# Six places in place of eight for the gathered rows of the value stage

## The reference, cut to what matters

```
act = jax.nn.gelu(jnp.einsum('td,thkd->thk', hx, u[ex]))
out = jnp.einsum('thk,thkd->td', (gx.astype(act.dtype) * act), v[ex])
```

## Time and profile before

| | |
|---|---|
| median of 3 runs | 1711.44 us (1711.39, 1711.44, 1716.0) |
| the profiled execution, its own time | 1713.18 us |
| its span, first to last instruction | 1711.3 us |
| granted TensorE clock, mean | 0.978 |
| PE busy | 1621.1 us (95%) |
| DVE busy | 1064.0 us (62%) |
| POOL busy | 619.8 us (36%) |
| queue q0, the gathers | 268.47 MB |
| queue q1, SP's transfers | 208.06 MB |

### The profile page before, as it was taken

The page is one execution under the profiler, slowest core; times in us unless marked ns, Lnnn a source line. Parts: engine busy times, 40 slices in busy tenths (PEclk is TensorE's granted clock), DMA queues, the critical chain, the costliest instruction groups (busy, mean ns, idle before and its releaser), DMA issues.

```text
span 1711.3 us, 18283 instructions
## 1 busy us (share of the span) xinstructions
PE 1621.1 (95%) x6294; PEld 1052.1 (61%) x6294; DVE 1064.0 (62%) x2428; ACT 431.0 (25%) x1255; POOL 619.8 (36%) x650
## 2 busy tenths in 40 slices
PE   6988999998999799999989999999999999999957
PEld 3446454446588488888879999994444444444323
DVE  1010344442236999999968999997555556676772
ACT  3000444332011112111147777760000000000013
POOL 0000344460000144344445555555443344464620
PEclk9997999999999899999999999999999999999979
DMA  6231211004444699999989999999999999999940
GB/s 219 74 111 49 87 50 38 25 1 148 148 135 136 236 355 350 379 398 365 372 330 408 403 403 402 407 402 407 409 409 409 410 409 409 409 409 410 410 197 37
DMA packets 132552, 477.69 MB, mean 279 GB/s; under 512 B 14779, under 2 KB 15803, under 8 KB 132460
## 3 DMA queue, kind: packets, MB, share of 16 engines
q0 software_dynamic: 73728, 268.47, 40.0%
q1 hardware_dynamic: 58732, 208.06, 32.6%
HBM read 472.24 MB, written 4.24 MB: 278 GB/s over the span
## 4 chain that ended last, share of the span: by engine, by line
PE 65%; DMA 24%; DVE 4%; POOL 3%; issue 2%; ACT 1%; another core or an unknown queue 1%; SPq 0%; ACTq 0%; DVEq 0%
PE psum L1542 25%; DMA arena<-in_v,eidx 22%; PE psum L1453 6%; PE psum L1382 6%; PE psum L1272 5%; PE psum L1531 3%; PE psum L1415 3%; PE psum L1403 3%; PE psum L1489 2%; POOL arena L523 2%; PE psum L1340 2%; PE psum L1355 2%; PE psum L1295 1%; PE psum L1326 1%; PE psum L1285 1%
## 5 line engine op out<-in xcount | busy, mean ns | idle before, releaser
L1542 PE MATMUL psum<-arena 128*128 128x256 f32 x2048 | 455.2, 380 | 6.8 <-ACT arena L682 6.1
L1553 PE MATMUL psum<-arena 128*128 128x512 f32 x1024 | 440.8, 592 | 3.3 <-DMA arena<-in_vd 2.2
L523 POOL DMA_INDIRECT arena<-in_u,eidx x256 | 252.9, 988 | 474.7 <-DVE dots L1075 238.9
L1542 PEld LDWEIGHTS psum<-arena 128*128 128x128 f32 x2048 | 385.4, 191 | 57.4 <-issue 6.5
L523 POOL DMA_INDIRECT arena<-in_v,eidx x256 | 259.6, 1014 | 264.3 <-DVE arena L1110 147.8
L1553 PEld LDWEIGHTS psum<-arena 128*128 128x128 f32 x1024 | 194.2, 190 | 248.7 <-issue 242.5
L1110 DVE SCALAR_TENSOR_TENSOR arena<-arena,wts 128x1024 f32<-128x1024 f32 x182 | 233.2, 1285 | 118.9 <-DMA arena<-in_v,eidx 117.5
L1075 DVE CUSTOM_DVE_ANT_0 arena<-psum,arena 128x1024 f32<-128x1024 f32 x256 | 299.5, 1220 | 1.3 <-DVE arena L946 0.3
L501 POOL TENSOR_SCALAR arena<-arena 128x256 f32<-128x256 f32 (+4 forms) x128 | 105.9, 847 | 282.2 <-DVE arena L842 224.6
L1382 PE MATMUL psum<-arena 128*128 128x512 f32 x256 | 118.4, 605 | 0.0
L1453 PE MATMUL psum<-arena 128*128 128x256 f32 x512 | 113.0, 379 | 1.5 <-ACT arena L612 1.5
(11 more groups left out here) (175 smaller groups left out, 1400.6 us busy)
## 6 DMA issues: line engine op xcount, KB each, us to landing
arena<-in_ut SPq DMA_DIRECT2D x128, 512.0 KB
arena<-in_vd SPq DMA_DIRECT2D x128, 512.0 KB
arena<-in_wpack SPq DMA_DIRECT2D x105, 512.0 KB
arena<-in_u,eidx POOLq DMA_INDIRECT x256
arena<-in_v,eidx POOLq DMA_INDIRECT x256
arena<-in_w_pg SPq DMA_DIRECT2D x8, 512.0 KB
arena<-in_x SPq DMA_DIRECT2D x4, 512.0 KB, 4.9
arena<-bias_rows SPq DMA_DIRECT2D x8, 256.0 KB, 5.6
```

The source lines that it names most:

```text
L523: G.indirect_dma_start(out=row_slot(n), out_offset=None, in_=a["v"] if values else a["u"], in_offset=bass.IndirectOffsetOnAxis(ap=eidx[:, ...
L1542: last = T.matmul(chunk_scores(c), u[:, k * P:(k + 1) * P], h2T1[:, k, :], start=(k == 0), stop=(k == KC - 1))
L1553: last = T.matmul(ps[VALUE_BANK[t] + h], mixed[:, c, t * P:(t + 1) * P], stream[:, c % SRING, h * HALF:(h + 1) * HALF], start=(c == 0), st ...
```

## The change

From row 272 on, the gathered rows use only the six places at `SL`. Gather n then takes place (n - 272) mod 6. Gathers from n = 278 on wait until row n - 6 was used, those before (from n = 8) until row n - 8 was used. The two waits for `dense_scores` fall away, since nothing is gathered to `H2` any more. The functions `slot_of` and `slot_uses` give the place and how often its semaphore has been raised.

```diff
         low_slots = NG * COLS + -(-early_sums // SLOTS) * SLOTS
-        vslots = slots[:SLOTS - 2] + [place(H2 + i * D, [D])[0] for i in range(2)]
+        LATE_SLOTS = SLOTS - 2
+
+        def slot_of(n):
+            return n % SLOTS if n < low_slots else (n - low_slots) % LATE_SLOTS
+
+        def slot_uses(n):
+            return n // SLOTS + 1 if n < low_slots else low_slots // SLOTS + (n - low_slots) // LATE_SLOTS + 1
 
         def row_slot(n):
-            return (slots if n < low_slots else vslots)[n % SLOTS]
+            return slots[slot_of(n)]
...
-                if n >= SLOTS:
+                if n >= low_slots + LATE_SLOTS:
+                    pool.wait_ge(row_used, n - LATE_SLOTS + 1)
+                elif n >= SLOTS:
                     pool.wait_ge(row_used, n - SLOTS + 1)
-                if low_slots <= n < low_slots + SLOTS and n % SLOTS >= SLOTS - 2:
-                    pool.wait_ge(dense_scores, CHUNKS)
                 G.indirect_dma_start(out=row_slot(n), out_offset=None, in_=a["v"] if values else a["u"],
                                      in_offset=bass.IndirectOffsetOnAxis(ap=eidx[:, col:col + 1], axis=0)
-                                     ).then_inc(row_gathered[n % SLOTS], 16)
+                                     ).then_inc(row_gathered[slot_of(n)], 16)
...
-                dve.wait_ge(row_gathered[n % SLOTS], 16 * (n // SLOTS + 1))
+                dve.wait_ge(row_gathered[slot_of(n)], 16 * slot_uses(n))
```

## The result

The changed kernel is slower: 1718.26 us (median of 20 runs, 1714.82 to 1723.03) against 1712.56 us for the kernel before (20 runs, 1710.30 to 1717.36), ratio 1.0030, 95% interval 1.0021 to 1.0038. The medians differ by 5.7 us; the ratio makes it 5.1 us in 1712. The forecast was 1712.2 with a range to 1717.1. The profiled execution of the changed kernel took 1719.07 us, its span is 1717.3 (before: 1713.18 and 1711.3).

The account below looks back on a forecast made before the run. The prediction took the full DMA engines, up to the sum of row k = 120, as the bound. Transition 0.8 us plus three terms of 0 on the 1711.44 us median gave 1712.2 us, range 1708.3 to 1717.1.

Parts of the forecast that it names:

- What bounds the kernel: Value stage: DMA engines full until row k = 120 of the last tile is summed; the kernel's end follows that row.
- The transition: Start of six places: gather 278 waits for row 272, starting about 2.2 us later; cost 0 to 1.6, taken as 0.8 us.
- Rival C: At gather 278: the removed wait for dense scores pays, up to 3.1 us come back, 1708.3 us; chance 0.07.
- The mixed stretch: 1165 to 1620 us, dense stream beside gathered rows: six places give 12.3 us per round at 2.05 us a row; cost 0.
- The rows-only stretch: 1620 to 1641 us, after the dense stream: six places give a 7.68 us round at 1.28 us a row; cost 0.
- the 4.5 us above: A row's round without queueing: sum 1.28, GpSimd's reaction 0.27, issue until first bytes 1.67, own transfer 1.28 us.
- the upper bound of 4.1 us: After the stream: the whole 7.79 us trip taken as fixed, 1.51 us per row, 4.1 us lost over 18 rows.
- A: After the stream: the gather's trip is latency, not queueing; 4.1 us lost there, 1716.3 us in all; chance 0.08.
- B: Value stage: with fewer rows on order, fast DMA engines run dry before slow ones free a place; 1720.9 us, chance 0.09.

Follow-up runs that it names:

- early_tail: Kernel before, eight places, with the dense tiles' adds moved ahead in VectorE's order (tile 2's after k = 106, tile 3's after k = 109): 1694.80 us against 1712.96, ratio 0.9894.

## Why the prediction was wrong

- *What bounds the kernel.* Right: the DMA is full up to row 120, and the end follows that row. 9.3 us more of lost DMA time less 1.9 us of an earlier start make 7.4 us, of which 6.7 are seen at row 120; early_tail shows the same path from the other side.
- *The transition, 0.8 us.* Right in mechanism and size: gather 278 is released by row 272, and 0.7 us is lost (0.2 in the kernel before). It starts at 1163.15, which is 1162.13 + 0.75 + 0.27. Rival C falls.
- *The mixed stretch, cost 0.* Right where there is a stream (0.1 us in 225). Wrong from 1498 to 1538, 2.7 us: I averaged rows over the whole stretch (2.05 us) and did not see that PE's gate product of tile 0 stops the stream for 17 us, and that the rows then come at 1.28 us. The trace of before showed it: 11 sums without a gap, 14.08 us from 1516.11.
- *The rows-only stretch, cost 0.* This is the step that failed: "Lower bound of the need: the 4.5 us above, so nothing is lost", and the upper bound of 4.1 us. Measured are 5.6 us of DMA time, with the rows 1.69 us apart from 1627.57 to 1646.19. Both bounds take the pace from the round of a place, as if GpSimd issued as soon as one is free. By that sum the measured trip would do: 6.14 + 1.28 + 0.27 = 7.7 us, six places, 1.28 us a row, nothing lost. But GpSimd didn't come round: its places stood free for 2.6 us while each gather took 0.98 us and the gap of VectorE's sums on top. The rows of before showed 0.94 to 0.98 us, and came from a stretch in which the two keep step. The 4.5 us was too small as well; alone a round is 5.79 us. What opens the first gaps is the depth (gather 493 waits 0.96 us for its place, its row is 1.00 us late): they are there with sums in PSUM too, where 2.3 us are lost with short gathers, and not with eight rows on order.
- *The rivals.* A expected sums over 1.35 us apart with GpSimd waiting for a place. The sums came 1.69 us apart, but GpSimd waited for none, and the trip had shrunk to 6.14 us; that A's 4.1 us come near the 5.6 is luck. B (uneven engines) was not tried; whether it has a part in the 2.3 us that are lost with short gathers is open.
- *The numbers.* The difference of 0.30% lies on the line of 0.3% that I drew for slower, and 1718.26 is 1.2 us over the range.

## What to carry to other kernels

A depth of buffers is measured where its consumer is alone on the resource, not by the mean over the stage: look for each stretch in which the competing stream pauses. A round per place bounds the pace only while the issuing engine is quick enough: look whether it waits for a place or is late by itself. And a duration read where two engines keep step is no bound for where they don't. Where GpSimd issues gathers beside VectorE sums in SBUF, look at the spread of the gathers' own durations first.

## What the runs showed of the hardware

- A gather issued by GpSimd takes 0.94 us; if it starts more than 0.1 us after a VectorE multiply-add whose operands all lie in SBUF has begun, and before that ends, it ends 0.82 us after it, up to 2.00 us in all (all 116 gathers from 1420 us to the sum of row 120, in the changed kernel and as many in the one before, within 0.1 us). With the sum in PSUM it is never stretched (28 of 28, and all gathers of four sections measured alone).
- VectorE is held up little in turn: a sum begun well inside a gather takes 1.28 us, one begun 0.05 to 0.1 us before a gather 1.30 to 1.35 us.
- After a gap g between two such sums, the gather behind it takes 0.98 + g us (seven of seven within 0.02).
- One gathered row of 512 KB with its sum, alone on the chip, has a round of 5.79 us; two in turn 2.85; the DMA's 1.28 us per row are reached with six places if the sums lie in PSUM (1.29), and not with ten in SBUF (1.45).
- Unbroken sums and free gathers fall into step after one stretched gather (1.36, then 0.94 us, 1.24 us apart).
